# A float32r kernel of two transformer blocks: the weight ring's tiles and the shared activation buffers start at other addresses

## The reference

```python
def _squared_relu_mlp(x, w1, w2):          # 1024 -> 4096 -> 1024, twice in the first block
    h = jax.nn.relu(x @ w1)
    return (h * h) @ w2

def first_block(x, ...):
    h = x
    for layer in range(DEPTH):             # 2
        xn = _rms_norm(h, norm_g[layer, 0])
        m = _even_mixer(xn, ...) if layer % 2 == 0 else _sgu_mixer(xn, ...)
        h = h + _rms_norm(m, norm_g[layer, 1])
        f = _squared_relu_mlp(_rms_norm(h, norm_g[layer, 2]), ffn_w1[layer], ffn_w2[layer])
        h = h + _rms_norm(f, norm_g[layer, 3])
    return h

def second_block(x, ...):
    h = layer_norm(x, ln0_g, ln0_b)
    proj = h @ w_in[l] + b_in[l]
    ...
    attn_out = mixed @ w_out[l] + b_out[l]
    h = layer_norm(DEEPNORM_ALPHA * h + attn_out, ln1_g[l], ln1_b[l])
    u = jnp.square(jax.nn.relu(h @ w_ff1[l] + b_ff1[l]))
    ffn_out = u @ w_ff2[l] + b_ff2[l]
    return layer_norm(DEEPNORM_ALPHA * h + ffn_out, ln2_g[l], ln2_b[l])
```

## Time and profile before

| what | value |
|---|---|
| median of 2 runs | 2053.26 us (2051.97 to 2054.56) |
| profiled execution, span from the first to the last instruction | 2050.8 us |
| instructions | 28847 |
| moved by DMA | 182.12 MB, 89 GB/s |

### The profile page before, as it was taken

One profiled execution on the slowest core, in us unless ns is written; L12 is line 12 of the kernel. 1 busy time (PEld: TensorE's weight loads), 2 busy tenths in 40 slices (PEclk: granted clock), 3 DMA queues, 4 the chain that ended last, 5 costly groups with the idle time before them and its releaser, 6 DMA issues.

```text
span 2050.8 us, 28847 instructions
## 1 busy us (share of the span) xinstructions
PE 2024.3 (99%) x11240; PEld 1711.9 (83%) x11240; DVE 1049.8 (51%) x1722; ACT 802.5 (39%) x1348; POOL 173.8 (8%) x160
## 2 busy tenths in 40 slices
PE   9999899999999999999999999999999999999998
PEld 7887788888889888889888888987888898888887
DVE  6557757344344736626443435727644544344344
ACT  7325645232233533323332323545554345223232
POOL 1001010200002001210120002300000210000000
PEclk9999999999999999999999999999999999999999
DMA  5222003232322322232323323232122313333321
GB/s 195 89 71 83 22 22 112 95 103 92 100 85 82 124 93 83 87 98 75 111 93 98 97 86 100 93 103 93 52 63 82 95 60 105 97 97 93 101 82 42
DMA packets 52047, 182.12 MB, mean 89 GB/s; under 512 B 5872, under 2 KB 8064, under 8 KB 51936
## 3 DMA queue, kind: packets, MB, share of 16 engines
q1 hardware_dynamic: 50112, 173.23, 27.0%
q0 software_dynamic: 1824, 7.32, 1.1%
HBM read 178.43 MB, written 2.10 MB: 88 GB/s over the span
## 4 chain that ended last, share of the span: by engine, by line
PE 92%; DVE 5%; ACT 2%; issue 1%; DMA 0%; POOL 0%; SPq 0%; ACTq 0%; DVEq 0%
PE ps L390 58%; PE ps L1099 5%; PE ps L469 4%; PE ps L508 3%; PE ps L1761 3%; PE ps L1838 3%; PE ps L1039 2%; PE ps L1082 2%; PE ps L1056 1%; PE ps L1749 1%; PE ps L1481 1%; PE ps L820 1%; PE ps L1459 1%; PE ps L1597 1%; DVE ring L363 1%; PE ps L1851 1%
## 5 line engine op out<-in xcount | busy, mean ns | idle before, releaser
L390 PE MATMUL ps<-xa,ring 128*128 128x512 f32 x3048 | 702.9, 391 | 0.0
L390 PEld LDWEIGHTS ps<-xa,ring 128*128 128x128 f32 x3048 | 570.1, 188 | 120.5 <-issue 2.7
L356 ACT ACTIVATE ring<-raw 128x1024 fp32r<-128x1024 f32 x320 | 336.6, 1054 | 485.7 <-PE ps L390 382.1
L363 DVE TENSOR_TENSOR ring<-raw,ring 128x1024 fp32r<-128x1024 f32 x320 | 402.2, 1259 | 204.6 <-ACT ring L356 204.1
L390 PE MATMUL ps<-xb,ring 128*128 128x512 f32 x2208 | 502.6, 389 | 0.0
L390 PEld LDWEIGHTS ps<-xb,ring 128*128 128x128 f32 x2208 | 414.4, 188 | 86.1
L945 DVE TENSOR_TENSOR ffsq<-relu 128x512 f32<-128x512 f32 x96 | 66.4, 691 | 178.7 <-ACT relu L904 178.7
L962 DVE TENSOR_TENSOR acc<-acc,ps 128x512 f32<-128x512 f32 x68 | 46.8, 688 | 196.3 <-PE ps L390 196.3
L904 ACT ACTIVATE relu<-ps 128x512 f32<-128x512 f32 x64 | 38.1, 596 | 185.0 <-PE ps L390 182.7
L948 DVE TENSOR_TENSOR xb<-ffsq,xb 128x512 fp32r<-128x512 f32 x96 | 66.5, 692 | 75.8 <-ACT xb L896 75.8
L1099 PE MATMUL ps<-xa,ring 128*128 128x512 f32 x432 | 104.3, 396 | 0.0
(11 more groups left out here) (371 smaller groups left out, 2065.4 us busy)
## 6 DMA issues: line engine op xcount, KB each, us to landing
raw<-in_stream SPq DMA_DIRECT2D x320, 512.0 KB, 3.5
t<-in_rpb POOLq DMA_DIRECT2D x8, 384.0 KB, 5.5
h<-in_x SPq DMA_DIRECT2D x8, 256.0 KB, 7.4
c_w<-in_cmp_w POOLq DMA_DIRECT2D x4, 512.0 KB, 4.1
out_y<-h SPq DMA_DIRECT2D x16, 128.0 KB, 1.9
cons<-in_con SPq DMA_DIRECT2D x1, 578.0 KB, 9.3
raw<-in_stream SPq DMA_DIRECT2D x2, 256.0 KB, 4.1
wst<-in_w_s POOLq DMA_DIRECT2D x1, 512.0 KB, 3.7
```

The costliest lines, as they stand in the source:

```text
L356: nc.scalar.activation(ring[:, m % RING, 0], raw[:, m % RING], ACT.Copy).then_inc(hi_done, 1)
L363: nc.vector.tensor_tensor(ring[:, m % RING, 1], raw[:, m % RING], ring[:, m % RING, 0].bitcast(F32), ALU.subtract).then_inc(lo_done, 1)
L390: mm = nc.tensor.matmul(bank[:, :], ring[:, n % RING, w, k * P:(k + 1) * P], operand[:, k, xx], start=(start and i == 0 and w == 0 and xx ...
```

## The change

`ring` gets 8 more elements (32 bytes) at the end of each of its eight tiles (`STEP`), so a tile is 4128 bytes apart from the next. They now start, in the order high and low of slots 0 to 3, at 128, 160, 192, 224, 0, 32, 64 and 96 modulo 256. The two splits name the 1024 elements that they write. What lies behind the ring up to the shared area moves by 256 bytes and keeps its place modulo 256. `shared` is raised to 192 modulo 256 in place of 128, so every tensor in it lies 320 bytes further on, 64 of them modulo 256. `h`, `xa` and `raw` stay where they are. No engine's list of instructions changes, neither in kind nor in order.

```diff
--- before.py
+++ after.py
@@ -33,6 +33,7 @@
 KC = D // P
 FF = 4 * D
 RING = 4
+STEP = 8
 AHEAD = 3
 NEG = -1e30
 HD = 64
@@ -236,7 +237,7 @@
         h = keep("h", [P, KC, T])
         xa = keep("xa", [P, KC, 2, T], F32R)
         raw = keep("raw", [P, RING, KC * P])
-        ring = keep("ring", [P, RING, 2, KC * P], F32R)
+        ring = keep("ring", [P, RING, 2, KC * P + STEP], F32R)
         xf_at = place[0]
         xf = keep("xf", [P, 4, T])
         sq_at = place[0]
@@ -255,7 +256,7 @@
         stat = keep("stat", [P, 16, 16])
         bn = keep("bn", [P, TB, 4, 6])
         bqa = keep("bqa", [P, 4])
-        shared = place[0] + (P - place[0]) % 256
+        shared = place[0] + (P + P // 2 - place[0]) % 256
 
         def at(name, shape, kb, dt=F32):
             assert shared + int(kb * 1024) + int(np.prod(shape[1:])) * 4 <= nc.sbuf_usable_end, name
@@ -353,15 +354,15 @@
             act.wait_ge(landed[m % RING], 16 * (m // RING + 1) + more)
             if m >= RING:
                 act.wait_ge(panel_done, m - RING + 1 + panels_more)
-            nc.scalar.activation(ring[:, m % RING, 0], raw[:, m % RING], ACT.Copy).then_inc(hi_done, 1)
+            nc.scalar.activation(ring[:, m % RING, 0, 0:KC * P], raw[:, m % RING], ACT.Copy).then_inc(hi_done, 1)
 
         def dve_split(dve, n, more=0):
             m = n + AHEAD
             if m >= NP:
                 return
             dve.wait_ge(hi_done, m + 1 + more)
-            nc.vector.tensor_tensor(ring[:, m % RING, 1], raw[:, m % RING], ring[:, m % RING, 0].bitcast(F32),
-                                    ALU.subtract).then_inc(lo_done, 1)
+            nc.vector.tensor_tensor(ring[:, m % RING, 1, 0:KC * P], raw[:, m % RING],
+                                    ring[:, m % RING, 0, 0:KC * P].bitcast(F32), ALU.subtract).then_inc(lo_done, 1)
 
         def pe_free_bank(pe, bank, n, more=0):
```

## The result

The changed kernel takes 2084.84 us (median of 2 runs, 2084.61 to 2085.06) against 2053.26 us: a ratio of 1.0159, 95% interval 1.0143 to 1.0176. That is under the 2% at which the forecast drew the line between "same" and "slower", but clear of the spread of the runs, and 19 us above the range that was given.

A forecast was written before the change was run, and what follows sets the result against it. The prediction took TensorE's matmuls to bound the kernel. Span 2050.8 us plus 0 each for TensorE, ACT and DVE, and DMA, plus 2.5 us around it, gave 2053.3 us, range 2040 to 2066.

The forecast's parts named there:

- What bounds the kernel: Whole kernel: matmuls fill 99% of the span at full clock; the chain is 92% PE, 5% DVE, 2% ACT, 0% DMA.
- the price of a nanosecond per matmul: All 8664 float32r matmuls, 6744 of 512 columns and 1920 of 256: one nanosecond on each is 8.7 us.
- TensorE's price: Float32r matmuls with new operand starts: between 85 us gained and 116 us lost, taken as 0.
- The outcome "same": Whole kernel: measured time within about 2%, 41 us, of no change; chance 0.85.
- The argument of the phases: Weight and moving streams in TensorE: new starts only shift streams of different length, so any meetings should already be mixed; supports 0.
- ACT, DVE and DMA at 0: Ring splits and loads: taken as 0, with 1.6 us up or down for ACT and DVE; DMA holds 0% of chain.
- Rival A: Float32r matmuls: operands starting equal modulo 256 cause the addition, 1/6 stay slow; gain 70.8 us, 1982 us; chance 0.06.
- Rival B: Weight fetches in 128-byte pieces: tiles off that grid cost 13.4 ns on 2/3 of matmuls; 77.4 us, 2131 us; chance 0.09.
- Case C: Float32r matmuls: starts off a finer grid cost or win 0.8 ns on 2/3, 4.8 us; chance within the 0.85.
- The range: Whole kernel: 2040 to 2066 us, from run spread, 1.6 us, 4.8 us and up to 1.5 ns per matmul, 13 us.
- sign of being wrong: TensorE's cadence moving by more than 4.7 ns on average, or the chain's share of DVE and ACT growing from 7%.
- the 3.6 ns: Plain fp32 matmuls at L820: their addition, 216.9 against 213.3 ns, assuming two clocks a column.

The follow-up runs named there:

- TensorE alone: Separate kernel without the computation: 48 matmuls per phase (weights' start minus moving operand's, modulo 256), 64 phases; bursts at 512 columns take 10.88 to 11.37 us.
- the halves: Against the kernel before, panels read by 256-column matmuls start 32 bytes sooner or 64, 76, 88 later in their slot: 2048.46, 2045.87, 2043.68, 2045.46 us.
- everything 64 bytes further: Against the kernel before, h, xa, raw, ring and shared area all start at 192 modulo 256, differences unchanged: 2051.94 us, ratio 1.0002.
- tile e: Ring tiles at 0 modulo 256 in the by-slot run; matmuls reading them show medians of 393 and 397 ns, against 389 before.
- the low-tile run: Against the kernel before, only the low ring tiles move, to 192 modulo 256; high tiles and shared area stay at 128: 2077.51 us, ratio 1.0124.
- the by-slot run: Against the kernel before, high and low tile of a slot start alike, slots 64 bytes apart, shared area at 160: 2081.31 us, ratio 1.0147.

## Why the prediction was wrong

**What bounds the kernel: right.** The chain, its shares and the count of 8664 matmuls held, and so, roughly, did the price of a nanosecond per matmul. By it the new cadences make 6744 x 5.8 - 1920 x 1.8 = 35.7 us; the span grew by 32.0, as some pieces lost less (with the ring moving 4.5 ns a matmul).

**TensorE's price: the step that failed.** The prediction bounded the price of a new start by -85 and +116 us and then took 0, "the value nearest to the rows". Measured were +5.8 ns at 512 columns and -1.8 ns at 256. The rows that spoke for 0 showed the cadence constant over slots, parts, blocks and buffers. But all those pairs have phase 0 (the blocks are 512 bytes apart, the rows 2048), so they are one point seen thousands of times, and say nothing of another. The exact 389/389/389 was no sign of indifference but of a rhythm that only a few phases have. The outcome "same", given 0.85, did come, but by luck: 32 us stayed under the line of 41 us for no reason that the prediction had.

**The argument of the phases: wrong.** It said that two streams which pass through all places modulo 256 must meet in a mixture, whatever their starts. TensorE alone shows the contrary: 226.9 ns at phase 0, 232.5 at 4 bytes. The starts do fix the rhythm.

**ACT, DVE and DMA at 0: right.** Medians of 1054 and 1224 ns, and 0% of DMA in the chain.

**Rival A** (equal starts cost) had the sign wrong for 512 columns: phase 0 is among the best there. It holds in a way at 256, where most phases beat phase 0, and that is why the halves gained. **Rival B** (a grid of 128 bytes) had the right sign, but its mechanism is refuted by everything 64 bytes further (off the grid, ratio 1.0002) and by tile e, on the grid and slow; its 77 us were also more than twice too many. **Case C** (small ticks off a fine grid) was nearest in kind, but no grid of starts is the cause, and it was mis-sized: 0.8 ns on two thirds, where 5.8 on the mean of 512 columns was measured.

**The range** allowed 1.5 ns per matmul either way and had no row behind it. With the bounds at -85 and +116 us it was far too narrow. It was narrower, too, than the prediction's own sign of being wrong, 4.7 ns on the average: the measured 35.7 us over 8664 matmuls are 4.1 ns, short of that sign and still outside the range.

**A misreading that changed little.** The 16 rows of L820 are 8 matmuls of two rows each, as TensorE alone shows (L206: 48 matmuls, 96 rows). So 216.9 ns is a row of a plain fp32 matmul and not a whole one, and the 3.6 ns taken from it, on which the bound of -85 us and rival A rest, are not the addition of a matmul like the others. No float32r matmul of any run came near it.

**The rules that were weighed.** The Trainium skill's page "SBUF — State Buffer" (section "Who interferes with whom") would have the change worth 0, as it gives TensorE two independent read ports. TensorE alone, with nobody beside it, differs by up to 11.37 - 10.88 = 0.49 us in 48 matmuls by the difference of two read addresses, so for float32r the measurement decides against the 0. It doesn't show that it is at the ports that the two reads meet. The 215.8 ns of the Trainium skill's page "TensorE: Matmul & The Clock Gate" (section "Back-to-back issue gap") come out for bfloat16, and in no phase for float32r.

**How the loss is made up.** With TensorE's own map, the change's high tiles meet xa at 0, 64, 128 and 192 (226.9, 233.1, 233.5 and 229.4 ns, mean 230.7) and its low ones at 32, 96, 160 and 224 (mean 233.5). Two thirds and one third are 231.6 ns, 4.7 more than phase 0's 226.9. The 232.5 of the change leave some 1 ns for the neighbours at other phases, which the low-tile run shows to exist; that the two parts simply add is an estimate. Where a panel has one phase only, the map alone is enough: for the by-slot run it gives (504 x 230.7 + 576 x 233.5) / 1080 = 232.2 ns, measured 250.66 / 1080 = 232.1. What in the chip makes the map, a clash of the weights' and the moving reads or something else that depends on both addresses, these runs don't tell.

## What to carry to other kernels

Where float32r matmuls bound a kernel, the difference modulo 256 between the starts of weights and moving operand is worth some 3% of a matmul at 512 columns and more at 256: keep it the same for all pairs, 0 at 512 columns, and measure the halves by themselves. Here that came to 1.6% of the kernel. Other phases than 0 that TensorE alone showed as good need a check in the kernel, with the ring moving as well (120 bytes). A number that is constant over thousands of rows says nothing of a change that moves a quantity which all those rows share; write down first what they have in common. And where an unknown has bounds of -4% and +6%, a range of 0.6% either way needs a row of its own.

## What the runs showed of the hardware

- The cadence of a float32r matmul depends on the phase to 4 bytes, without order: 226.7 to 236.9 ns at 512 columns over 64 phases, 113.3 to 133.3 ns at 256. It needs no other engine.
- 128 x 256 matmuls at phases 28, 32 and 36 take 133.1 to 133.3 ns, 17% more than at 64 (113.5).
- Plain fp32 (215.8 ns a row at 256 columns) and bfloat16 (215.8 ns at 512) show none of it at the phases tried (0, 4, 64 and 128 bytes).
- ACT's and DVE's splits of 1024 elements keep their medians with the ring's tiles at all eight multiples of 32 bytes modulo 256: 1054 against 1053 ns and 1224 against 1224.
